# Two trunk layers on one core: six of branch D's eight gate products put between the attention's steps, their logits parked in DRAM, and D's remaining products put together

## The chip, the cores and the metric

One core of one Trainium2 chip runs the whole kernel. The metric is the device time of one execution in microseconds, as the median of the runs shown. TensorE is written PE, VectorE DVE, ScalarE ACT and SyncE SP, as the profile does; GpSimd does nothing here beyond two memsets at the start.

## The reference, cut to what matters

Two layers are applied to 640 tokens (512 latent, 128 context). In each layer one wide projection of the normed input `h` feeds four mixers; each mixer's output is projected to the model's width and weighted by a gate that is computed from the same `h`:

```
z = h @ p['w_in']                       # the last 4 * 1024 columns are merge_logits
y_a, y_c   attention (A: 4 heads of 64; C: differential, 8 score maps of 32)
y_b, y_d   chunkwise linear attention (HGRN2, GLA)
branches = jnp.stack([y_a, y_b, y_c, y_d], axis=2)
proj  = jnp.einsum('btnw,nwd->btnd', branches, p['w_branch'])
gates = jax.nn.sigmoid(merge_logits.reshape(bsz, t, N_BRANCH, D_MODEL))
mixed = jnp.sum(gates * proj, axis=2) @ p['w_out']
x = x + g1 * mixed
x = x + g2 * conv_ffn(...)
```

A gate of one branch for 128 output channels is a product of 1024 x 128 weights with `h` (8 blocks of 128 in depth); the branch's projection for these channels is a product over 256 (2 blocks). `y_d` is the last branch to be ready. The gates of D need only `h`, which is ready before the attention.

## The kernel before

Channels lie on the 128 partitions, the 640 tokens along the free axis. The kernel is written by hand, engine by engine, with semaphores; nothing is scheduled by a compiler, and each engine works through its instructions in the order of the code. For each of two layers: the projections of the mixers (`z`), the attention, then the stage in which B and D are computed while PE fills its waits with the gate and branch products of A, C and B (24 "mix" units, `MERGE`), then D's own gates and branches ("D's stage"), the output projection (`out`), and the ConvFFN (`up`, `down`).

A product is done in split precision: each weight block and each input block is a rounded part ("hi") plus the rest ("lo"), and `block_product` (L571 to L573) issues hi x hi, hi x lo and lo x hi for each of two halves of 320 tokens, six matmuls for a block of depth. So a gate is 48 matmuls of 320 columns, a D branch product 12. For every weight unit ACT makes the hi part (`mix_unit` L1137, `out_unit` L1216) and DVE the lo part (`lo`, L1432) before PE can start on it. Weights come by SP's queue through a ring of four slots (`RING`); SP waits for a free slot before each load, and what stands behind that wait on the queue waits too.

The attention has 30 steps `g` in a layer (five blocks of 128 queries, six steps each: two for A, four for C); the last six have 128 keys only, the others 768. `scores` (L712, L714) writes two score maps into two PSUM pairs and waits until ACT has taken the two maps of the step before. `maxima` (DVE L1511), `exponentials` (ACT L1114), `normalise` (DVE L1518 to L1524), `turn` (PE transposes, L725), `keep_turned` (ACT L1124) and `weigh` (PE, probabilities times values, L739) follow at a distance of up to three steps. In one step PE issues scores(g), turn(g-3, second map), turn(g-2, first map), weigh(g-3); DVE issues maxima(g), then normalise(g-1). `outputs` (L1529) copies the attention's result out of PSUM. `ATT_OUT` takes both banks of the fourth pair.

D's stage before: for each `j` of eight groups of 128 channels PE does the gate and then the branch product; ACT takes the sigmoid from PSUM (L1231); DVE multiplies (`merge`, L1704), adds it to the sum (L1710), ACT rounds that (`round_mixed`, L1235) and DVE makes its rest (`mixed_rest`, L1715). The `out` products read the rounded sum and the rest.

## Time and profile before

| | before |
|---|---|
| median of 3 runs | 2751.46 us (2750.52 to 2757.59) |
| the profiled execution: time, span | 2750.94 us, 2749.2 us |
| mean granted clock of TensorE | 0.956 |
| attention, layer 0: first maxima to last step with 768 keys | 333.61 to 461.33 us |
| D's stage, layer 0 | 788.48 to 858.88 us |
| `out` products, layer 0 | 858.88 to 915.30 us |

Times in the rows are microseconds from the first instruction. In a timeline row stand the start, the duration, the engine and line, what is written and read, how many instructions are merged, and in square brackets how long the engine sat idle before it and what it had waited for. PE's matmuls overlap, so its own pace is read from start to start. A window row gives busy time (and instruction counts) of PE, weight loads, DVE, ACT and POOL, then the granted clock, the DMA share and GB/s.

### The profile page before, as it was taken

What the parts mean: (1) busy time and instruction counts of PE and PEld (TensorE: products, weight loads), DVE (VectorE), ACT (ScalarE), POOL (GpSimd) and SP (SyncE); (2) the same over time, 40 slices, a digit from 0 to 9 for tenths busy, and PEclk for the clock granted to TensorE, in tenths of its full rate; (3) what the DMA queues carried; (4) which work ended last, traced back from release to release, by engine and by line L of the source; (5) the groups of instructions that cost most, each with busy time, mean ns of one, the idle gap of its engine ahead of it and who ended that gap; (6) DMA issues with size and microseconds to landing.
All of it is one profiled execution on the core that took longest, in us unless ns stands there. A gap on an engine that the chain in (4) does not pass through costs nothing.

```text
span 2749.2 us, 43334 instructions
## 1 busy us (share of the span) xinstructions
PE 2541.6 (92%) x18502; PEld 2356.8 (86%) x18502; DVE 1336.9 (49%) x2037; ACT 939.9 (34%) x1306; POOL 2.2 (0%) x6
## 2 busy tenths in 40 slices
PE   4999877999999899998989997879999989999898
PEld 2988655888999899998989884568899989999898
DVE  3123266886644545554231324678775445555521
ACT  4134345222142532333242434542213334233411
POOL 0000000000000000000000000000000000000000
PEclk7999878999999999999999997999999999999999
DMA  8445200221233122222244340011222322222121
GB/s 292 156 143 183 82 1 1 52 54 50 58 99 102 55 70 76 76 62 81 74 146 127 100 144 26 1 29 49 51 63 72 121 62 62 77 76 72 54 74 70
DMA packets 322759, 222.77 MB, mean 81 GB/s; under 512 B 17520, under 2 KB 320688, under 8 KB 321712
## 3 DMA queue, kind: packets, MB, share of 16 engines
q1 hardware_dynamic: 317200, 203.45, 25.4%
q10 hardware_dynamic: 5408, 17.13, 1.7%
q8 instruction: 116, 1.90, 0.3%
q14 instruction: 35, 0.29, 0.0%
HBM read 211.51 MB, written 9.04 MB: 80 GB/s over the span
## 4 chain that ended last, share of the span: by engine, by line
PE 85%; DVE 5%; ACT 5%; issue 2%; DMA 1%; SPq 0%; ACTq 0%; POOLq 0%; DVEq 0%; POOL 0%
PE PS L571 23%; PE PS L573 23%; PE PS L572 23%; PE PS L817 3%; PE PS L739 2%; PE PS L712 2%; PE PS L725 2%; PE PS L595 2%; PE PS L560 1%; DVE RING_split L1432 1%; PE PS L714 1%; ACT HH_split L983 1%; PE PS L853 1%; DVE NMX L1511 1%; ACT WORK L985 1%
## 5 line engine op out<-in xcount | busy, mean ns | idle before, releaser
L571 PE MATMUL PS<-HH_split,WHI_split 128*128 128x320 f32 x3552 | 1119.7, 315 | 44.7 <-DVE HL_split L1418 17.7
L573 PE MATMUL PS<-HH_split,RING_split 128*128 128x320 f32 x3552 | 1103.6, 311 | 0.0
L572 PE MATMUL PS<-HL_split,WHI_split 128*128 128x320 f32 x3296 | 1024.5, 311 | 0.0
L571 PEld LDWEIGHTS PS<-HH_split,WHI_split 128*128 128x128 f32 x3552 | 673.0, 189 | 66.9 <-issue 57.3
L573 PEld LDWEIGHTS PS<-HH_split,RING_split 128*128 128x128 f32 x3552 | 672.6, 189 | 0.0
L572 PEld LDWEIGHTS PS<-HL_split,WHI_split 128*128 128x128 f32 x3296 | 625.1, 190 | 2.4 <-issue 2.4
L1432 DVE TENSOR_TENSOR RING_split<-RING,WHI_split 128x1024 fp32r<-128x1024 f32 (+2 forms) x200 | 274.4, 1373 | 499.7 <-ACT WHI_split L1220 230.6
L572 PE MATMUL PS<-ZT_split,WHI_split 128*128 128x320 f32 x1216 | 378.0, 311 | 0.0
L572 PEld LDWEIGHTS PS<-ZT_split,WHI_split 128*128 128x128 f32 x1216 | 230.6, 190 | 0.0
L1220 ACT ACTIVATE WHI_split<-RING 128x1024 fp32r<-128x1024 f32 x88 | 93.3, 1060 | 290.6 <-PE PS L573 290.6
L571 PE MATMUL PS<-V_split,WHI_split 128*128 128x320 f32 x544 | 172.3, 317 | 19.9 <-DVE ZT_split L1787 15.1
L1439 DVE TENSOR_TENSOR RING_split<-RING,WHI_split 128x1024 fp32r<-128x1024 f32 x54 | 64.2, 1222 | 250.1 <-ACT WHI_split L1001 250.0
L573 PE MATMUL PS<-V_split,RING_split 128*128 128x320 f32 x544 | 170.3, 313 | 0.0
L1511 DVE TENSOR_REDUCE NMX<-PS 128x1 f32<-128x768 f32 (+1 forms) x120 | 93.3, 819 | 102.2 <-PE PS L714 91.7
L1173 ACT ACTIVATE WHI<-PS 128x640 f32<-128x640 f32 x48 | 33.9, 705 | 280.6 <-PE PS L573 280.4
L1114 ACT ACTIVATE BIG<-PS,NMX 128x768 f32<-128x768 f32 (+1 forms) x120 | 94.1, 791 | 88.3 <-DVE NMX L1511 88.3
L571 PEld LDWEIGHTS PS<-V_split,WHI_split 128*128 128x128 f32 x544 | 104.3, 192 | 22.2 <-issue 20.8
L1591 DVE COPY_PREDICATED BIG<-MASK,PS 128x640 f32<-128x640 uint8 x112 | 98.1, 882 | 51.8 <-PE PS L817 51.0
L1224 ACT ACTIVATE WHI_split<-RING 128x1408 fp32r<-128x1408 f32 x32 | 44.2, 1380 | 226.0 <-PE PS L573 226.0
L1137 ACT ACTIVATE WHI_split<-RING 128x1280 fp32r<-128x1280 f32 x64 | 81.5, 1273 | 83.0 <-PE PS L573 83.0
L712 PE MATMUL PS<-ZT 32*128 32x512 f32 (+1 forms) x192 | 65.0, 758 | 45.3 <-ACT BIG L1114 44.0
L573 PEld LDWEIGHTS PS<-V_split,RING_split 128*128 128x128 f32 x544 | 104.3, 192 | 0.0
(181 smaller groups left out, 2781.8 us busy)
## 6 DMA issues: line engine op xcount, KB each, us to landing
RING<-in_w_in SPq DMA_DIRECT2D x112, 512.0 KB, 4.0
RING<-in_w_ada SPq DMA_DIRECT2D x96, 512.0 KB, 6.0
RING<-in_w_up SPq DMA_DIRECT2D x88, 512.0 KB, 5.0
RING<-in_w_down SPq DMA_DIRECT2D x32, 384.0 KB, 3.6
RING<-in_w_down SPq DMA_DIRECT2D x32, 320.0 KB, 4.0
RING<-in_w_branch SPq DMA_DIRECT2D x64, 128.0 KB, 4.1
RING<-in_w_out SPq DMA_DIRECT2D x16, 512.0 KB, 4.1
x_kept<-BIG ACTq DMA_DIRECT2D x2, 2560.0 KB, 9.8
```

The costliest lines, as they stand in the source:

```text
L571: release(pe.matmul(out, w_hi, hi[:, a:b], start=begin, stop=False), fresh and a == 0)
L572: pe.matmul(out, w_hi, lo[:, a:b], start=False, stop=False)
L573: ins = pe.matmul(out, w_lo, hi[:, a:b], start=False, stop=end)
L712: pe.matmul(pair(m)[:, 0:TS], ZT[r[m], q, ti], ZT[r[m], k, 0:TS], start=True, stop=True)
L817: last = pe.matmul(pair(3 - e)[:, ti], KM[p % 2][r, ti], QM[p % 2][r, ti], start=True, stop=True)
L1114: act.activation(PROB[g % 3][m][:, 0:n], pair(m)[:, 0:n], ACT.Exp, bias=NMX[:, g % 3, m:m + 1], accum_out=SUMS[:, g % 3, m:m + 1]).then_in ...
L1137: act.activation(W2[m % 2][:, 0:1280], RING[:, (MIX + m) % N_SLOT, 0:1280], ACT.Copy).then_inc(hi_made, 1)
L1220: act.activation((w or W2[h])[:, 0:1024], RING[:, (UP + j) % N_SLOT, 1024 * h:1024 * h + 1024], ACT.Copy).then_inc(hi_made, 1)
L1432: nv.tensor_tensor(rest, value, as_f32(hi), ALU.subtract).then_inc(lo_made, 1)
L1439: nv.tensor_tensor(z_raw(RING_R, l, c, j), z_raw(RING, l, c, j), as_f32(tiles_of(W4[u % LEAD])), ALU.subtract).then_inc(lo_made, 1)
L1511: nv.tensor_reduce(NMX[:, g % 3, m:m + 1], pair(m)[:, 0:keys(g // NS) * P], AX.X, ALU.max, negate=True).then_inc(nmax_ready, 1)
L1591: ins = nv.copy_predicated(SCORE[:, h], m, ps)
```

## The change

- The gates of D for the first six channel groups (`N_EARLY`) are computed during the attention. `gate_parts` splits each into two halves of 320 tokens, each a chain of 8 units of three matmuls, accumulated in `HALF_GATE`, 320 columns of the second bank of the fourth pair. `GATE_FILL` says how many units PE issues at two places of a step: 2, 6, 2 and 6 units in four steps, 96 units over the 24 steps with 768 keys. ACT copies each half (the logits, no sigmoid yet) to SBUF (`gates_kept`), and PE waits for that copy (`half_kept`) before it begins the next half.
- SP stores each gate's logits to DRAM (`send_gate`), and loads the six back near the end of D's computation.
- The attention's outputs share the first bank of that pair; `weigh` of A waits for `outputs` of the C part before it, and of C for those of A.
- In the attention the transposes run one step earlier: turn(g-2, second), weigh(g-3), turn(g-1, first); DVE does normalise(g-1) before maxima(g). DVE also makes the lo part of a gate's weights (`early_lo`), ACT the hi part (`early_unit`).
- D's stage is ten products: two gates (groups 6 and 7), then eight branch products from two 512-column loads of `w_branch`. The gates that come from DRAM get their sigmoid in SBUF. `merge` no longer has weights to split between its two operations, and SP starts to load `w_out` only when `merge` has used the four gates that lie in the ring (`gate_used`).
- The first two `out` products run together, block by block (`two_products`), and wait for the lo part of the second one's weights. `out` has three hi buffers instead of two.

```diff
+GATE_FILL = ((0, 2), (4, 2), (1, 1), (1, 5))
...
+def halves_before(g):
+    return min(2 * N_EARLY, sum(sum(GATE_FILL[i % 4]) for i in range(g)) // KT)
...
-        ATT_OUT = PS[:, 3, :].rearrange("p (b a t) -> p b a t", b=2, t=P)
+        ATT_OUT = PS[:, 3, 0:512].rearrange("p (b a t) -> p b a t", b=2, t=P)
+        HALF_GATE = PS[:, 3, 512:512 + HALF]
...
+                gate_chunk(LAST, 6)
+                sp.wait_ge(ko_turned, l * 6 + 6)
+                for n in range(N_EARLY):
+                    sp.wait_ge(gate_sent[n], l * 16 + 16)
+                    sp.dma_start(GATE_D[n], LOGITS[:, n, :]).then_inc(gates_in, 16)
+                gate_chunk(LAST + 1, 7)
...
+                sp.wait_ge(gate_used, l * 4 + 4)
                 for c in range(4):
                     slot_free(OUT + c)
                     columns(w_out, (OUT + c) % 4, 256 * c, 256)
...
+                def gate_parts():
+
+                    for n in range(N_EARLY):
+                        w_hi, w_lo = tiles_of(W_EARLY), raw(RING_R, EARLY + n, 0, P, P, KT)
+                        for h, (a, b, _) in enumerate(HALVES):
+                            if h == 0:
+                                lo_ready(U_MIX + n)
+                            if n + h:
+                                pe.wait_ge(half_kept, l * 2 * N_EARLY + 2 * n + h)
+                            for k in range(KT):
+                                release(pe.matmul(HALF_GATE, w_hi[:, k, :], h_hi(k)[:, a:b], start=k == 0, stop=False), h + k == 0)
+                                pe.matmul(HALF_GATE, w_hi[:, k, :], h_lo(k)[:, a:b], start=False, stop=False)
+                                ins = pe.matmul(HALF_GATE, w_lo[:, k, :], h_hi(k)[:, a:b], start=False, stop=k == KT - 1)
...
-                    if g >= 3:
-                        turn(g - 3, 1)
-                    if 0 <= g - 2 < NG:
-                        turn(g - 2, 0)
-                    if g >= 3 and (g - 3) % NS not in (2, 4):
-                        weigh(g - 3)
+                    turn(g - 2, 1)
+                    weigh(g - 3)
+                    gate_fill(g, 0)
+                    turn(g - 1, 0)
+                    gate_fill(g, 1)
...
+                for j in range(KT):
+                    g, at = G_D + 2 + j, j % 4 * P
+                    wait_room(pe, l, g)
+                    if j % 4 == 0:
+                        lo_ready(U_D + 2 + j // 4)
+                    product(use(g)[0], tiles_of(W2[j // 4][:, 0:1024], 512)[:, :, at:at + P], raw(RING_R, LAST + 2 + j // 4, at, P, 512, 2),
...
+                lo_ready(U_OUT + 1)
+                two_products(G_OUT, [out_weights(0), out_weights(1)], m_ready, m_hi, m_lo)
...
+                        if h and n + 1 < N_EARLY:
+                            early_unit(n + 1)
+                        if n == 4 and h == 0:
+                            act.wait_ge(gate_sent[0], l * 16 + 16)
+                        act.activation(LOGIT[n][:, HALVES[h][0]:HALVES[h][1]], HALF_GATE, ACT.Copy).then_inc(half_kept, 1)
...
                 for j in range(KT):
-                    gate(j, 0)
-                    wait_event(act, l, EV_D + 2 * j + 1)
-                    if j < 6:
-                        mix_unit(N_IN + j + 2)
-                    else:
-                        out_unit(j - 6)
+                    if j % 4 == 3:
+                        wait_event(act, l, EV_D + 2 + j)
+                        out_unit(j // 4)
                     round_mixed(j, M_HI[j])
...
                 v.wait_ge(al_ready, l * 2 + 2)
+                early_lo(0)
+                early = 1
                 for g in range(NG + 1):
-                    if g < NG:
-                        maxima(g)
-                    if g >= NS and g % NS == 3:
+                    while early < N_EARLY and 2 * early <= halves_before(g - 1):
+                        early_lo(early)
+                        early += 1
+                    if g % NS == 5:
+                        outputs(g // NS, 0)
+                    if g > NS and g % NS == 3:
                         outputs(g // NS - 1, 1)
                     if g:
                         normalise(g - 1)
-                    if g % NS == 5:
-                        outputs(g // NS, 0)
+                    if g < NG:
+                        maxima(g)
...
+                    step.mark(nv.tensor_tensor(GATED, GATE_D[j], acc(p), ALU.mult))
+                    step.settle(v)
+                    v.sem_inc(gemm_free[p], 1)
+                    if j < 4:
+                        v.sem_inc(gate_used, 1)
                     link(nv.tensor_tensor(dst, dst, GATED, ALU.add))
...
                 for j in range(KT):
                     merge(j)
+                    if j % 4 == 3:
+                        out_lo(j // 4)
                     mixed_rest(j, M_HI[j])
+                out_lo(2)
```

On PE, step g = 4 of the attention before holds the scores, two transposed maps and one product with the values:

```order
L712 MATMUL PS<-ZT 128x512 x2
L714 MATMUL PS<-CACHE,ZT 128x256 x2
L725 MATMUL PS<-CONST,BIG 128x128 x12
L739 MATMUL PS<-WHI,V 64x128 x8
L739 MATMUL PS<-WHI,CACHE 64x128 x4
```

and the same step now:

```order
L762 MATMUL PS<-ZT 128x512 x2
L764 MATMUL PS<-CACHE,ZT 128x256 x2
L793 MATMUL PS<-WHI,V 64x128 x8
L793 MATMUL PS<-WHI,CACHE 64x128 x4
L777 MATMUL PS<-CONST,BIG 128x128 x6
L807 MATMUL PS<-HH_split,WHI_split 128x320
L808 MATMUL PS<-HL_split,WHI_split 128x320
L809 MATMUL PS<-HH_split,RING_split 128x320
L807 MATMUL PS<-HH_split,WHI_split 128x320
L808 MATMUL PS<-HL_split,WHI_split 128x320
L809 MATMUL PS<-HH_split,RING_split 128x320
```

Two units of a gate end the step, and one of the two maps is turned in another step than before. On DVE, the same place before is maxima(4), then normalise(3):

```order
L1511 TENSOR_REDUCE NMX<-PS 128x1 x2
L1518 RECIPROCAL RCP<-SUMS 128x2
L1523 TENSOR_SCALAR BIG<-BIG,RCP,NLAM 128x768
L1524 SCALAR_TENSOR_TENSOR BIG<-BIG,RCP 128x768
```

and now, from maxima(4) to maxima(5):

```order
L1624 TENSOR_REDUCE NMX<-PS 128x1 x2
L1545 TENSOR_TENSOR RING_split<-RING,WHI_split 128x1024
L1645 COPY ZT<-PS 128x2x128
L1634 RECIPROCAL RCP<-SUMS 128x2
L1639 TENSOR_SCALAR BIG<-BIG,RCP,NLAM 128x768
L1640 SCALAR_TENSOR_TENSOR BIG<-BIG,RCP 128x768
L1624 TENSOR_REDUCE NMX<-PS 128x1 x2
```

The lo part of the second gate's weights (L1545) stands behind maxima(4), though PE's step 4 above already reads it; normalise(4) stands ahead of maxima(5). On DVE in D's stage, two groups of channels before:

```order
L1704 TENSOR_TENSOR WORK<-WHI,PS 128x640
L1432 TENSOR_TENSOR RING_split<-RING,WHI_split 128x1280
L1710 TENSOR_TENSOR ZT<-ZT,WORK 128x640
L1715 TENSOR_TENSOR ZT_split<-ZT,V_split 128x640
L1704 TENSOR_TENSOR WORK<-WHI,PS 128x640
L1432 TENSOR_TENSOR RING_split<-RING,WHI_split 128x1280
L1710 TENSOR_TENSOR ZT<-ZT,WORK 128x640
L1715 TENSOR_TENSOR ZT_split<-ZT,V_split 128x640
```

and now groups 2 and 3:

```order
L1831 TENSOR_TENSOR WORK<-RING,PS 128x640
L1836 TENSOR_TENSOR ZT<-ZT,WORK 128x640
L1841 TENSOR_TENSOR ZT_split<-ZT,V_split 128x640
L1831 TENSOR_TENSOR WORK<-RING,PS 128x640
L1836 TENSOR_TENSOR ZT<-ZT,WORK 128x640
L1545 TENSOR_TENSOR RING_split<-RING,WHI_split 128x8x128
L1841 TENSOR_TENSOR ZT_split<-ZT,V_split 128x640
```

The splits between the multiplications and the additions are gone, but that of `w_out` for the first `out` product (L1545 with 128x8x128) stands inside the chain at group 3, ahead of the rest of the sum.

## Rows read from the trace of the kernel before

**Rows 1.** The page: its head and its first part.

```profile
span 2749.2 us, 43334 instructions
...
PE 2541.6 (92%) x18502; PEld 2356.8 (86%) x18502; DVE 1336.9 (49%) x2037; ACT 939.9 (34%) x1306; POOL 2.2 (0%) x6
```

**Rows 2.** Windows of layer 0: attention's first twelve steps, D's stage, `out`.

```profile
330.90:368.74 37.84, 24.77 (x130) 14.68 (x127) 19.50 (x29) 17.25 (x34) 0.00 (x0) 0.67 0.03 11
368.74:399.60 30.86, 24.59 (x192) 16.64 (x193) 21.12 (x33) 16.86 (x33) 0.00 (x0) 0.89 0.00 1
...
788.48:858.88 70.40, 70.40 (x483) 70.40 (x482) 32.45 (x35) 25.58 (x29) 0.00 (x0) 1.00 0.42 132
858.88:915.30 56.42, 56.42 (x386) 56.30 (x384) 22.37 (x30) 14.27 (x16) 0.00 (x0) 1.00 0.26 75
```

**Rows 3.** Timeline of one attention step, all engines.

```profile
404.93 1.13 PE L712 MATMUL PS<-ZT 64*128 64x512 f32 x4
...
406.43 0.87 PE L725 MATMUL PS<-CONST,BIG 128*128 128x128 f32 x6
406.53 1.82 DVE L1511 TENSOR_REDUCE NMX<-PS 128x1 f32<-128x768 f32 x2 [1.00 <-PE PS L714]
...
409.45 1.13 PE L712 MATMUL PS<-ZT 32*128 32x512 f32 x4 [2.15 <-ACT BIG L1114]
```

**Rows 4.** Timeline of a step of C: a turned map, normalise, weigh.

```profile
418.13 0.84 PE L725 MATMUL PS<-CONST,BIG 128*128 128x128 f32 x6 [0.99 <-ACT WHI L1124]
418.43 0.15 DVE L1518 RECIPROCAL RCP<-SUMS 128x2 f32<-128x2 f32 x1
...
418.90 1.09 PE L739 MATMUL PS<-WHI,V 128*64 128x128 f32 x16
419.34 1.02 DVE L1524 SCALAR_TENSOR_TENSOR BIG<-BIG,RCP 128x768 f32<-128x768 f32 x1
...
420.37 1.13 PE L712 MATMUL PS<-ZT 32*128 32x512 f32 x4
```

**Rows 5.** PE's timeline where 320-column matmuls meet others.

```profile
507.28 0.31 PE L573 MATMUL PS<-HH_split,RING_split 128*128 128x320 f32 x1
507.52 1.39 PE L817 MATMUL PS<-RING,BIG 64*128 64x128 f32 x20
508.84 0.42 PE L571 MATMUL PS<-HH_split,WHI_split 128*128 128x320 f32 x1
509.09 0.31 PE L572 MATMUL PS<-HL_split,WHI_split 128*128 128x320 f32 x1
```

**Rows 6.** Timeline at the start of the attention.

```profile
332.11 1.47 ACT L1106 ACTIVATE ZT<-BIG 128x640 f32<-128x640 f32 x2 [0.27 <-DVE BIG L1506]
333.61 1.82 DVE L1511 TENSOR_REDUCE NMX<-PS 128x1 f32<-128x768 f32 x2 [0.80 <-ACT ZT L1106]
```

**Rows 7.** Timeline of PE after its long wait behind `out`.

```profile
927.33 0.60 PE L571 MATMUL PS<-HH_split,WHI_split 128*128 128x320 f32 x1 [5.78 <-DVE HL_split L1418]
...
932.97 0.30 PE L571 MATMUL PS<-HH_split,WHI_split 128*128 128x320 f32 x1
```

**Rows 8.** Timeline of DVE and ACT in D's stage.

```profile
797.63 0.82 DVE L1704 TENSOR_TENSOR WORK<-WHI,PS 128x640 f32<-128x640 f32 x1 [2.32 <-PE PS L573]
...
800.27 0.82 DVE L1710 TENSOR_TENSOR ZT<-ZT,WORK 128x640 f32<-128x640 f32 x1
801.95 0.83 DVE L1715 TENSOR_TENSOR ZT_split<-ZT,V_split 128x640 fp32r<-128x640 f32 x1 [0.86 <-ACT V_split L1235]
...
859.16 1.06 ACT L1216 ACTIVATE WHI_split<-RING 128x1024 fp32r<-128x1024 f32 x1 [1.05 <-PE PS L573]
...
860.25 1.23 DVE L1432 TENSOR_TENSOR RING_split<-RING,WHI_split 128x1024 fp32r<-128x1024 f32 x1 [0.20 <-ACT WHI_split L1216]
```

**Rows 9.** The page: a copy out of PSUM, and loads by SP.

```profile
L1173 ACT ACTIVATE WHI<-PS 128x640 f32<-128x640 f32 x48 | 33.9, 705 | 280.6 <-PE PS L573 280.4
...
RING<-in_w_out SPq DMA_DIRECT2D x16, 512.0 KB, 4.1
```

More of the change, by code:

```diff
@@ L741, in weigh, with gate_fill @@
                     last.then_inc(pv_done, 1)
+                def gate_parts():
+                    for n in range(N_EARLY):
+                        w_hi, w_lo = tiles_of(W_EARLY), raw(RING_R, EARLY + n, 0, P, P, KT)
[8 more added lines that the diff above has]
+                                ins = pe.matmul(HALF_GATE, w_lo[:, k, :], h_hi(k)[:, a:b], start=False, stop=k == KT - 1)
+                                if k == KT - 1:
+                                    ins.then_inc(half_gate, 1)
+                                yield
+                gates = gate_parts()
+                def gate_fill(g, n):
+                    for _ in range(GATE_FILL[g % 4][n]):
+                        next(gates, None)
                 for g in range(NG + 3):
@@ L890, in _, with m_hi, m_lo @@
+                def m_hi(k):
+                    return M_HI[k]
+                def m_lo(k):
+                    return ZT_R[:, MIXT + k, :]
+                lo_ready(U_OUT + 1)
+                two_products(G_OUT, [out_weights(0), out_weights(1)], m_ready, m_hi, m_lo)
+                for t in range(2, 8):
+                    wait_room(pe, l, G_OUT + t)
+                    lo_ready(U_OUT + t)
+                    product(use(G_OUT + t)[0], *out_weights(t), m_hi, m_lo, KT, t % 2 == 0)
                 mean_square(1)
```

200 lines of the change are left out of this document (123 added, 77 removed).

## The prediction

> **What bounds the kernel now.** I read the page first: PE is busy for 92% of the span, DVE for half of it [rows 1]. Then the windows by stage. In D's stage and in `out` PE is busy without a gap at the full clock; in the attention the granted clock is 0.67 in the first six steps and 0.89 in each later six [rows 2]. So what D's stage loses in PE work it can lose in time, as long as nothing else becomes late there, and the attention is the place with slack. How much, the step's timeline tells: scores start at 404.93, the next at 409.45, and PE had sat idle for 2.15 us, waiting for ACT's second map [rows 3]. These 4.5 us are a loop of latencies: scores 1.6, two maxima 1.82 with ACT half a map behind, ACT's two maps.
>
> **PE's work in six steps, at full clock.** Scores take 1.5 us (404.93 to 406.43) [rows 3]. A turned map is 0.77 (418.13 to 418.90), a `weigh` 1.47 (418.90 to 420.37) [rows 4]. Six steps hold 6 scores, 8 maps and 4 `weigh`: 9.0 + 6.2 + 5.9 = 21.1 us, in a stretch of 30.86 [rows 2]. Slack 9.8.
>
> **What the fill costs.** D's stage is 480 matmuls of 320 columns in 70.40 us [rows 2], so 0.147 each; a unit of three is 0.44, and six steps get 24 units, 10.6 us. Each group of units put between other matmuls also pays for the meeting: L573 to L817 is 0.24 and L571 to L572 behind it 0.25, against 0.147, so 0.2 for both ends [rows 5]. There are 7 groups in four steps, 10.5 in six: 2.1 us. Together 21.1 + 10.6 + 2.1 = 33.8, above 30.86: **PE becomes the bound of the attention**, and six steps last 2.9 us longer. Below stands 31.7 (+0.8), if the fp32 matmuls of the attention meet the units without a price. The loop that ruled before does not rule any more: from ACT's last map normalise of C takes 1.93 (418.43 to 420.36) [rows 4], then maxima(g) and ACT's maps 2.9, so 4.9 a step at most, against PE's mean of 5.6. A half copy of 320 columns is less than the 0.70 of 640 [rows 9], and ACT does it while PE does the next scores (1.5 us), before the next unit needs the bank; if that cover were gone it would be up to 0.7 for each of 12.
>
> Two smaller terms. (a) DVE makes a gate's lo weights behind maxima(g) of the step whose end PE wants to fill: maxima end 1.6 + 1.8 = 3.4 after the scores began, lo is 1.23 [rows 8], ready at 4.7, while PE is there at 1.5 + 1.47 + 0.77 = 3.7, or at 4.5 where a second map is turned. Of the five places three cost 1.0 and two 0.25: 3.5. (b) At the start `early_unit` (1.06) and `early_lo` (1.23) [rows 8] stand between the last ACT operation of the decays and the first maxima, at 333.61 with no other wait [rows 6]: +2.5, so scores(1) at 339.1. Step 1 holds scores, one map and six units with two meetings: 1.5 + 0.8 + 2.6 + 0.4 = 5.3. Step 2 has two units only, so the loop rules: 4.9. Step 3 has both maps, a `weigh` and six units: 7.6. Step 4 has a map, a `weigh`, two units and 1.0 of (a): 5.8. Step 5 is as step 1: 5.3. Together 28.9, and the clock is low at first. After PE's wait behind `out` it stays at half for 5.64 us of work (927.33 to 932.97, 0.267 a matmul) [rows 7], a loss of at most 2.8; I take 2.2. Then step 6 begins at 370.2, against 368.74: +1.5, with the gain from a clock that was 0.67 in it. The later three stretches: 3 x 2.9 = 8.7, and the other 2.5 of (a). The last, short steps have no units: 0. **Attention: +12.7 us a layer** (between 0, where the clock's gain covers the units, and +16).
>
> **D's stage.** Six gates of 48 matmuls leave it: 288 x 0.147 = 42.2 us of PE. What is late next is DVE. PE's two gates run from 788.48 to 802.6. Then ACT's hi of the second branch chunk (1.06) and DVE's lo (1.23) [rows 8] stand ahead of all merges in DVE's order: first merge at 805.1. A group costs DVE: multiply 0.82, 0.06 to settle, 1.68 from the addition's start to that of the rest (800.27 to 801.95, ACT's rounding in it), 0.75 of the rest: 3.3 us [rows 8]. PE needs 12 x 0.147 = 1.8. Before, a gate's 7 us hid this chain; now it is bare. At group 3 comes a wait: SP loads `w_out` only after merge(3) has multiplied (815.0 + 0.9), each load lands after 4.1 [rows 9] and the second is issued 0.4 later, so 820.5; then ACT's hi to 821.6, DVE's lo to 822.9, the rest to 823.7. Group 4 starts at 823.6 in place of 818.3. ACT and DVE stand in order behind that load, so nothing goes round it. Groups 5, 6 and 7 start at 826.9, 830.2 and 833.5; the addition of 7 ends at 835.2, and then DVE makes the lo part that PE waits for ahead of the first two `out` products: 836.4. PE was last needed at 818, when group 3's multiplication had freed the PSUM pair of group 7. It restarts at 836.5 instead of 858.88: 22.4 us earlier, with 18 us of idleness behind it, so again 2.2 for the clock. Both products then run as before, the remaining six too. **D's stage: -20.2 us a layer.** Bounds: -25.5, if the load were hidden; -17, if the load lands 3 us later.
>
> The Trainium skill (TensorE: Matmul & The Clock Gate, Why this matters for your kernels) says to leave no long idle gaps between bursts, since PE then falls back to the low clock. That speaks against this change, which makes one such gap in D's stage and fills many in the attention; the rows agree (0.89 in the attention, the half-speed start above). By the rule alone the first products of `out` would be slow, which the sum has.
>
> The stores and loads of the logits (six of 320 KB each way) cost nothing: SP has them in stages where DMA share is 0 to 0.4 [rows 2], and the loads are issued when the last group's `KO` is turned, some 30 us ahead of their sigmoid. If they were late, ACT would be, and merge(0) behind it. The sigmoids themselves (0.7 each) end at about 806, as the first merge does. Outputs in one bank add waits of `weigh` for a copy of 0.4 us that DVE has made one step before: 0.
>
> **Sum.** A layer: +12.7 - 20.2 = -7.5; two layers -15.0. The profiled execution took 2750.94 (span 2749.2 [rows 1]), 0.5 below the median. 2750.9 - 15.0 = 2735.9, forecast **2736 us**.
>
> **Rivals.**
> 1. The units go in nearly free: no price for meetings, the higher clock pays the start; +3 a layer in place of +12.7. For it: the clock of 0.67 and 0.89, which leaves 4 to 8 us a layer to win. Against: PE's sum is above the stretch even at full clock. 2750.9 - 2 x 17.2 = 2716.5.
> 2. D's stage stays bound by PE (DVE's chain hidden, `w_out` in time): -42.2 there and +12.7: 2 x -29.5, so 2692. Against: 3.3 us a group in order on DVE against 1.8 on PE. It would need rounding and rest to overlap with the next group's multiplication, which the code's order forbids.
> 3. Slower, by one mechanism: the single bank of the halves. If ACT's copy waits behind its two maps (2 x 0.9 and two read-outs of 0.2) and PE for it, each of 12 boundaries costs 2.2 + 0.5. It decides from 7.5/12 = 0.6 us a boundary on. At 2.0 each: 24 a layer, 2750.9 + 2 x (24 - 7.5) = 2784. Against: in ACT's order the copy stands ahead of the step's maps, and a half ends with a step, so the scores cover it. The Trainium skill (Perfetto Trace Analysis, Matmuls) would expect this cost: "Independent matmul groups should rotate through different PSUM banks", so that the copy of one overlaps the next group's matmuls. No row here shows such a wait.
> 4. No difference: the attention becomes 18 to 22 us longer a layer, because 2, 6, 2, 6 units meet the steps with maps and `weigh` unevenly, so that latencies rule the short steps and PE the long ones (7.6 beside 4.9): 2746 to 2754. If the clock stays at 0.9 as well, 33.8 becomes 37.6 in each of four stretches, 15 a layer: 2766.
>
> **How the numbers follow.** The first sum with its own bounds (attention +9 to +15, D's stage -17 to -22): 0.57, from 2725 to 2746. Rival 1: 0.20. Rival 2: 0.04. Rival 3: 0.05. Rival 4: 0.14. The range of 8 in 10 goes from rival 1's time to just short of rival 4's middle: 2714 to 2750. A difference under 0.3% (8 us) is about what cannot be told from none; the first case reaches a little into it (from 2743 on). Rival 4 gives most of the chance of no difference and 0.03 of slower. Faster 0.78, same 0.14, slower 0.08.
>
> **What would show it.** Right: in the attention a granted clock near 1 and six steps in about 33.8 us, long steps every second, PE's waits small and for DVE's lo weights; in D's stage DVE at 3.3 us a group with one wait of about 5 us for `w_out` at group 3, PE idle for some 18 us ahead of the first `out` product, which starts 48 us after the start of D's stage instead of 70. Wrong: PE idle in the attention for ACT's half copies (rival 3), six steps still in 31 us (rival 1), steps longer than PE's own sum (rival 4), or PE busy through D's stage (rival 2).

## The result, and the profile after

The changed kernel takes 2723.8 us (median of four runs, 2722.7 to 2725.4) against 2751.3 before: a ratio of 0.9895, 95% interval 0.9883 to 0.9907. Forecast were 2736 us and a range of 2714 to 2750. The direction and the range held; the middle was 12 us too high. The kernel before was measured again beside each group of experiments (2753.6 to 2754.9 us), so where two versions differ by a few us their ratios to it say more than their times; one of the four executions of experiment 2, at 5359 us, is twice as long as the other three and is left out of its ratio.

The page of the changed kernel, head and first part, which answer to [rows 1]:

```profile
span 2723.6 us, 43386 instructions
...
PE 2523.2 (93%) x18502; PEld 2344.4 (86%) x18502; DVE 1339.8 (49%) x2041; ACT 948.4 (35%) x1334; POOL 2.2 (0%) x6
```

PE's matmuls are the same 18502 instructions, in 25.6 us less. Windows of layer 0, which answer to [rows 2]: the attention in four stretches of six steps, D's stage up to the first `out` product, and from there to PE's first product behind `out` (3.7 us of it a wait; measured to the same place, 919.12, the kernel before took 60.2 us where [rows 2] has 56.42). Columns: stretch, its length, busy time and number of instructions of PE, weight loads, DVE, ACT and POOL, granted clock, DMA share, GB/s.

```profile
329.72:369.11 39.39, 32.91 (x210) 23.87 (x210) 23.58 (x34) 23.21 (x41) 0.00 (x0) 0.87 0.16 46
369.11:401.38 32.27, 32.27 (x265) 25.02 (x264) 22.68 (x34) 19.05 (x37) 0.00 (x0) 1.00 0.09 28
401.38:435.43 34.05, 32.51 (x265) 24.99 (x264) 23.93 (x35) 20.15 (x38) 0.00 (x0) 1.00 0.21 59
435.43:467.70 32.27, 32.27 (x266) 25.01 (x265) 22.67 (x34) 19.05 (x37) 0.00 (x0) 1.00 0.11 32
796.86:846.28 49.42, 28.67 (x195) 28.14 (x193) 28.42 (x35) 21.28 (x28) 0.00 (x0) 0.85 0.38 132
846.28:909.04 62.76, 59.08 (x385) 58.84 (x385) 22.07 (x32) 15.27 (x18) 0.00 (x0) 0.96 0.24 68
```

In two of the three later stretches of the attention PE is now busy from end to end, at a granted clock of 1.00, where it was 0.89 in [rows 2]. A stretch grew from 30.9 us to 32.3 (34.1 in the third, which has two waits for weights). D's stage gives its time back: 49.4 us to the first `out` product in place of 70.4. Of these, PE works 28.7. PE's waits in the attention, in the changed kernel (who waited for whom, us in total, times, the longest):

```profile
PE PS L807 <- DVE RING_split L1545: 6.3, 4, 4.0
PE PS L759 <- ACT BIG L1220: 1.4, 3, 0.7
PE PS L762 <- ACT BIG L1220: 1.2, 2, 0.8
```

L807 is the first matmul of a unit, RING_split the lo part of its weights. It waits for DVE's lo weights and never for ACT's copy of a finished half. The 4.0 us are the first gate's, at the start; the three others are 0.8 each. Two smaller waits of PE (for a kept map and for the decays) are not shown.

DVE's, ACT's and SP's timeline in D's stage of the changed kernel, at group 3, with the restart of PE:

```profile
823.91 0.81 DVE L1831 TENSOR_TENSOR WORK<-RING,PS 128x640 f32<-128x640 f32 x1
824.90 3.56 SPq L486 DMA_DIRECT2D RING<-in_w_out  x6
824.96 0.83 DVE L1836 TENSOR_TENSOR ZT<-ZT,WORK 128x640 f32<-128x640 f32 x1 [0.24 <-DVE WORK L1831]
829.99 1.06 ACT L1329 ACTIVATE WHI_split<-RING 128x1024 fp32r<-128x1024 f32 x1 [6.85 <-DMA RING<-in_w_out]
831.15 1.23 DVE L1545 TENSOR_TENSOR RING_split<-RING,WHI_split 128x1024 fp32r<-128x1024 f32 x1 [5.36 <-ACT WHI_split L1329]
...
833.03 0.81 DVE L1831 TENSOR_TENSOR WORK<-WORK,PS 128x640 f32<-128x640 f32 x1
...
845.01 1.22 DVE L1545 TENSOR_TENSOR RING_split<-RING,WHI_split 128x1024 fp32r<-128x1024 f32 x1
...
846.28 0.64 PE L621 MATMUL PS<-V_split,WHI_split 128*128 128x320 f32 x1 [19.43 <-DVE RING_split L1545]
```

It reads from the top: group 3 has multiplied, SP may load `w_out` (824.90), it lands 5.1 us later, ACT makes hi, DVE has stood for 5.36 us and makes lo, and group 4 starts at 833.03. PE has stood for 19.43 us when the second unit's lo is there.

**Where the 25.6 us of span came from**, by the places where PE starts a stage in both traces (`ffn` is PE's first block product behind `out`):

| stretch | layer 0: before, after | layer 1: before, after |
| --- | --- | --- |
| decays' product to first mix product (attention) | 157.26, 162.73: +5.5 | 158.00, 162.43: +4.4 |
| first mix product to the second pause of the mix stage | 157.21, 159.37: +2.2 | 157.32, 157.25: -0.1 |
| from there through D's stage and `out` to `ffn` | 287.73, 268.53: -19.2 | 287.60, 268.57: -19.0 |

These sum to -26.2, and the rest of the span adds 0.6. Of the gain in the last row 18.5 and 18.1 us lie in D's stage and `out`, the rest behind them. The two layers do not divide the attention's growth alike: in layer 0 the part up to the seventh scores is 0.4 us shorter and the three later stretches are 6.0 longer; in layer 1 they are 2.2 and 3.8 longer (one of the stretches before lasted 33.0 there, at a clock of 0.84), and what follows them is 1.5 shorter.

### The profile page after: what moved, and what is told of

Same layout as the page of the kernel before. It is cut to its first block, busy times and chain, and to the rows that moved or that the text cites. A ratio compares the mean times of both kernels' runs of the same rounds, so it can differ in the third digit from the quotient of the medians.

```text
span 2723.6 us, 43386 instructions
## 1 busy us (share of the span) xinstructions
PE 2523.2 (93%) x18502; PEld 2344.4 (86%) x18502; DVE 1339.8 (49%) x2041; ACT 948.4 (35%) x1334; POOL 2.2 (0%) x6
## 4 chain that ended last, share of the span: by engine, by line
PE 83%; DVE 7%; ACT 6%; issue 2%; DMA 1%; SPq 0%; ACTq 0%; POOLq 0%; DVEq 0%; POOL 0%
PE PS L621 22%; PE PS L622 21%; PE PS L623 21%; PE PS L896 2%; PE PS L762 2%; DVE RING_split L1545 2%; PE PS L645 2%; PE PS L777 2%; PE PS L793 2%; PE PS L807 1%; PE PS L610 1%; ACT HH_split L1070 1%; ACT WORK L1072 1%; PE PS L809 1%; PE PS L808 1%
## 5 line engine op out<-in xcount | busy, mean ns | idle before, releaser
L621 PE MATMUL PS<-HH_split,WHI_split 128*128 128x320 f32 x3360 | 1061.2, 316 | 45.1 <-DVE HL_split L1531 18.3
L623 PE MATMUL PS<-HH_split,RING_split 128*128 128x320 f32 x3360 | 1044.4, 311 | 0.0
L622 PE MATMUL PS<-HL_split,WHI_split 128*128 128x320 f32 x3104 | 965.6, 311 | 0.0
L621 PEld LDWEIGHTS PS<-HH_split,WHI_split 128*128 128x128 f32 x3360 | 637.0, 190 | 68.4 <-issue 57.2
L623 PEld LDWEIGHTS PS<-HH_split,RING_split 128*128 128x128 f32 x3360 | 636.8, 190 | 0.0
L622 PEld LDWEIGHTS PS<-HL_split,WHI_split 128*128 128x128 f32 x3104 | 589.2, 190 | 2.4 <-issue 2.4
L1545 DVE TENSOR_TENSOR RING_split<-RING,WHI_split 128x1024 fp32r<-128x1024 f32 (+2 forms) x204 | 274.9, 1349 | 535.6 <-ACT WHI_split L1333 240.8
L1248 ACT ACTIVATE WHI_split<-RING 128x1280 fp32r<-128x1280 f32 (+1 forms) x56 | 69.5, 1241 | 78.1 <-PE PS L623 78.1
L1898 DVE SCALAR_TENSOR_TENSOR WORK<-PS,COLS,WORK 128x511 f32<-128x511 f32 (+1 forms) x176 | 88.6, 545 | 10.8 <-DVE WORK L1894 2.1
```

The costliest lines, as they stand in the source:

```text
L621: release(pe.matmul(out, w_hi, hi[:, a:b], start=begin, stop=False), fresh and a == 0)
L622: pe.matmul(out, w_hi, lo[:, a:b], start=False, stop=False)
L623: ins = pe.matmul(out, w_lo, hi[:, a:b], start=False, stop=end)
L1248: act.activation(W2[m % 2][:, 0:width], RING[:, (MIX + m) % N_SLOT, 0:width], ACT.Copy).then_inc(hi_made, 1)
L1545: nv.tensor_tensor(rest, value, as_f32(hi), ALU.subtract).then_inc(lo_made, 1)
L1898: ins = nv.scalar_tensor_tensor(out=c[:, a:b - 1], in0=u[:, a + 1:b], scalar=COLS[:, bass.ds(col + C_W2, 1)], in1=c[:, a:b - 1], op0=ALU.m ...
```

## The experiments

**1. Loads by slot.** Each chunk of `w_out` waits only for the gate that lies in its own slot; the four gates that come back into the ring are put in the slots in which `w_out` will arrive in order.

```
-        GATE_D = [RING[:, b, 1280:1280 + T] for b in range(4)] + ...
+        GATES_D = [[RING[:, (CHUNK0[l] + C_OUT + b) % N_SLOT, 1280:1280 + T] for b in range(4)] + ...
...
-                sp.wait_ge(gate_used, l * 4 + 4)
                 for c in range(4):
+                    sp.wait_ge(gate_used, l * 4 + c + 1)
```

> Edit: the four gates that lie in the ring are put where the four w_out chunks will go, in the order in which they are used, and each w_out load waits for its own slot's gate alone (chunk c for merge(c)), not for all four. Theory (the chain on DVE rules D's stage, with one wait of about 5.6 us for w_out at group 3): the first load starts behind merge(0) instead of merge(3), is there long before group 3, group 4 starts some 5.3 us earlier and so do the out products: out starts about 44 us after the start of D's stage in place of 49.4, 2 x 5.3 = 10.6 us in all, 2713. Rival (out's start is set by something else, ACT's hi parts or the PSUM pairs): out starts at 49 us again, 2724.

Measured: 2713.0 us, ratio 0.985 (0.9834 to 0.9867). D's stage up to the first `out` product, by windows, 5.3 us shorter:

```profile
795.43:839.53 44.10, 28.67 (x195) 28.14 (x194) 28.43 (x35) 21.16 (x28) 0.00 (x0) 0.90 0.43 148
```

So the wait for `w_out` at group 3 stood on the path with its whole length, 10.6 us in two layers, and it is avoidable.

**2. The second unit of `w_out` two groups earlier,** at group 5, on top of 1 ("version 2" below; the others are numbered alike).

```
-                    if j % 4 == 3:
-                        wait_event(act, l, EV_D + 2 + j)
+                    if j in (3, 5):
+                        wait_event(act, l, EV_D + (5 if j == 3 else 9))
                         out_unit(j // 4)
```

> Edit: on top of the loads by slot, the hi and lo parts of the second out product's weights are made at group 5 of D's stage instead of group 7. Theory: PE waits for that lo part alone, then takes six blocks of the two products whose sums are ready, and the last two are ready by the time it comes to them: out starts two groups earlier (6.8 us), the end of the two products moves as much, 2 x 6.7 = 13 us below the run with the loads by slot, about 2700. Rival (the rounded sums of groups 6 and 7 come too late, so PE only waits inside the products): the end of the two products moves by less than 3 us a layer, 2707 to 2713.

Measured: 2694.9 us, ratio 0.9783 (0.9763 to 0.9802). The same window, and PE's row behind it:

```profile
792.17:829.49 37.32, 28.66 (x195) 28.14 (x193) 23.65 (x29) 19.22 (x25) 0.00 (x0) 0.97 0.49 174
```

```profile
829.49 0.64 PE L622 MATMUL PS<-V_split,WHI_split 128*128 128x320 f32 x1 [7.33 <-DVE RING_split L1546]
```

Another 6.8 us a layer, two groups of DVE at 3.4, so 13.6 in all. The time fell by 18: in the two profiled executions, 16.9 us apart, the rest lies in stretches that the edit doesn't touch and that differ by 0.9 to 1.5 us each, most of them in favour of this version (the stretch from the last pause of the mix stage to D's stage: 150.42 us in version 1, 148.90 here). The restart hung on the place of one lo unit in DVE's order, and not on the mixed tiles: PE takes these one by one.

**3. No fill.** The 96 units run in a row behind the attention.

```
-GATE_FILL = ((0, 2), (4, 2), (1, 1), (1, 5))
+GATE_FILL = ((0, 0),) * 4
```

> Edit: no unit of a gate stands between the attention's steps, all 96 run behind the last step. Theory (with units PE's own sum rules the steps, without them the loop of latencies does, 4.5 us where the step before is A's and 4.9 where it is C's): six steps last 28.5 us in place of 32.9 with the units and 30.9 before the change. The 96 units take 42 us plus a bare copy of a half (0.7) at 12 places and bare hi and lo parts (2.4) at 5: 63. So +45 a layer, about 2815. Rival (the new order of transposes and normalise gives nothing): six steps take 31 us as before the change, about 2835.

Measured: 2850.8 us (two runs), ratio 1.0351 (1.0327 to 1.0375), 36 us more than expected. Windows of the later three stretches:

```profile
367.74:400.35 32.61, 26.39 (x193) 17.21 (x193) 21.50 (x33) 16.96 (x33) 0.00 (x0) 0.84 0.00 1
400.35:429.14 28.79, 21.71 (x192) 14.36 (x192) 21.41 (x33) 16.84 (x33) 0.00 (x0) 1.00 0.01 1
429.14:461.77 32.63, 26.42 (x193) 17.24 (x193) 21.50 (x33) 16.97 (x33) 0.00 (x0) 0.84 0.01 1
```

The 28.5 us that I expected of six empty steps are there once (28.8), at the full clock; in the two others the clock was 0.84 and they take 32.6, as long as six steps filled with 24 units (32.3). From the first scores to the twenty-fifth, the layer is 131.96 us without units and 137.98 with them: 42 us of PE's work are done for 6. The kernel before took 132.18, so the new order in the steps by itself shortened nothing. The rest of the miss is the row of units: 461.77 to the first mix product at 552.74 is 90.97 us, against 20.90 in the changed kernel, so 70 for the units, with 2.4 us for the lo weights of each gate but the first and half clock behind four of these five pauses:

```profile
514.95 0.64 PE L807 MATMUL PS<-HH_split,WHI_split 128*128 128x320 f32 x1 [2.40 <-DVE RING_split L1545]
```

**4. One place a step.** The same units, 4.5 meetings fewer in six steps.

```
-GATE_FILL = ((0, 2), (4, 2), (1, 1), (1, 5))
+GATE_FILL = ((0, 2), (0, 6), (0, 2), (0, 6))
```

> The changed kernel with the numbers of units per place at 0,2 | 0,6 | 0,2 | 0,6 in place of 0,2 | 4,2 | 1,1 | 1,5: the same 24 units in six steps, but one group of units a step instead of up to two, so 4.5 meetings fewer in six steps. Theory (a meeting of units with the attention's matmuls costs PE about 0.04 us): between -2 and +2 us over the whole kernel, 2724. Rival (0.2 us each, as predicted): 4.5 x 0.2 = 0.9 us less in each of the stretches, 3.6 a layer, so 7 us faster, 2717. A small loss would come from steps in which PE has nothing to put before the second turned map and waits for it.

Measured: 2723.4 us, ratio 0.9892 (0.9876 to 0.9909): no difference from the changed kernel. Windows of the three later stretches:

```profile
368.94:401.31 32.37, 32.09 (x265) 24.81 (x265) 22.97 (x34) 19.13 (x37) 0.00 (x0) 1.00 0.11 28
401.31:435.15 33.84, 32.29 (x265) 24.81 (x264) 23.64 (x35) 19.73 (x37) 0.00 (x0) 1.00 0.21 59
435.15:467.51 32.36, 32.07 (x265) 24.79 (x265) 22.97 (x34) 19.14 (x37) 0.00 (x0) 1.00 0.11 32
```

They sum to 98.6 us, as in the changed kernel. PE's busy time in the three fell from 97.05 to 96.45, 0.60 for 13.5 meetings: 0.04 each. (A meeting is one group of units between other matmuls.) Even that is not saved, since PE now stands as long elsewhere, twice for a normalised map (0.3 each):

```profile
PE PS L777 <- DVE BIG L1640: 0.6, 2, 0.3
```

As a net price of a meeting the rival's 0.2 is out; what the 0.04 is made of stands in the section on the prediction.

**5. Four units in every step.**

```
-GATE_FILL = ((0, 2), (4, 2), (1, 1), (1, 5))
+GATE_FILL = ((0, 4), (2, 2), (1, 3), (1, 3))
```

> Edit: the 96 units are spread evenly, four in each step, instead of 2, 6, 2, 6. Theory (a step lasts as long as the longer of PE's work and the loop of 4.5 to 4.9 us): the light steps (one map, no weigh) have 4.1 us of PE work and fall under the loop, the heavy ones get longer, six steps 33.3 in place of 32.1 (without the waits for lo weights): +4.7 a layer, about 2733. Rival (the unevenness of the steps, 4.7 beside 7.3, is what costs time against PE's sum): six steps get shorter, down to 31.7, about 2718.

Measured: 2727.8 us (two runs), ratio 0.9904 (0.9884 to 0.9924), between the two expectations. It is 4 us above the changed kernel, but the intervals of the two ratios overlap, so only the windows can tell them apart. The first of its later stretches, and PE's waits in the three of them:

```profile
365.82:398.89 33.07, 32.38 (x264) 24.99 (x264) 22.72 (x34) 19.03 (x37) 0.00 (x0) 1.00 0.09 27
```

```profile
PE PS L762 <- ACT BIG L1220: 2.0, 6, 0.3
PE PS L807 <- DVE RING_split L1545: 1.8, 2, 1.0
```

Six times PE waits 0.3 us for ACT's exponentials in a step of 4.51 us, the shortest there is: steps with one map and no `weigh` have too little work with four units. The changed kernel has six there and no such wait in these stretches. They sum to 101.2 us in place of 98.6; the first stretch is 1.6 shorter. The uneven 2, 6, 2, 6 of my rival 4 is thus the better spread in the later stretches; over the whole kernel the runs do not show it.

**6. The copy behind the exponentials,** which is rival 3's mechanism.

```
-                    gates_kept(halves_before(g))
                     keep_turned(g - 2, 1)
                     if g < NG:
                         exponentials(g)
+                    gates_kept(halves_before(g))
```

> The changed kernel with ACT's copy of the finished half of logits behind the step's two exponentials instead of ahead of them. This makes the third rival of the prediction true on purpose. Theory (the single bank of halves costs nothing only because ACT copies while PE does the scores): the copy is made about 2.2 us later, so PE, which wants the bank at once behind the scores and the turned map, waits about 1.8 to 2.0 us at each of 12 half boundaries: about 42 us in two layers, 2766. Rival (the place of the copy doesn't matter, since units have other slack): 2724.

Measured: 2811.7 us (two runs), ratio 1.0211 (1.0191 to 1.0232), 88 us slower than the changed kernel. PE's waits over the stretch that was shown above for the changed kernel:

```profile
PE PS L807 <- DVE RING_split L1545: 15.2, 5, 4.0
PE PS L807 <- ACT WORK L1211: 10.0, 5, 3.0
```

PE waits 2.0 us for a copy on average, as expected, at five places. What I had left out: the call that I moved also makes the next gate's hi weights, so at the four other places DVE's lo comes late (2.8 us on average); and the granted clock over 329 to 380 us is 0.71 where the changed kernel has 0.87 over its first six steps. So the experiment moves two things, and its 88 us are not the price of the copy alone. The place of this call decides between 28 us gained and 58 lost.

**7. Maxima first,** DVE's order of before.

```
+                    if g < NG:
+                        maxima(g)
                     if g % NS == 5:
                         outputs(g // NS, 0)
...
                     if g:
                         normalise(g - 1)
-                    if g < NG:
-                        maxima(g)
```

> The changed kernel with DVE's order in a step of the attention as it was before the change: maxima of this step ahead of the normalising of the step before. Theory (with units between, PE no longer waits for the exponentials but for the normalised map, which it turns in the same step; with the maxima ahead it comes 1.8 us later, and the PE's mean step of 5.4 us has no room for that): about 9 us more in each six steps, 72 in two layers, 2796. Rival (the order is free, since PE has units to do while DVE works): under 10 us more, 2724 to 2734.

Measured: 2833.3 us (two runs), ratio 1.029 (1.0269 to 1.031): 110 us slower than the changed kernel, where 72 were expected. PE's waits from 330 to 480 us:

```profile
PE PS L777 <- DVE BIG L1640: 18.9, 10, 3.4
PE PS L777 <- DVE BIG L1637: 6.4, 5, 2.0
```

L777 turns a map, L1637 and L1640 normalise it. The fifteen waits are 1.7 us each on average, as the theory said (1.8); the first to the twenty-fifth scores (328.5 to 514.6 us) take 186.1 us in place of 138.0. Over all of it the waits for a map sum to 30.8 us, those of `weigh` for DVE's `outputs`, which now stand behind the maxima, to 4.6, and the clock is 0.78, 0.89, 0.96 and 0.96 in the four stretches; the expectation had counted the first of these alone. With units in the steps, DVE's new order is a condition of the gain.

**8. The second unit at group 4,** on top of 2.

```
-                    if j in (3, 5):
-                        wait_event(act, l, EV_D + (5 if j == 3 else 9))
+                    if j in (3, 4):
+                        wait_event(act, l, EV_D + (5 if j == 3 else 9))
```

> On top of the version with w_out loaded slot by slot and the second unit of w_out at group 5: now that unit's hi on ACT and its lo on DVE stand at group 4. Theory (PE's restart in D's stage is set by where DVE makes the second unit's lo weights, and DVE's order of groups at 3.4 us each does the rest): out starts 3.4 us earlier a layer (its pause of 7.3 us becomes 3.9), and each k step of the first two products still finds its mixed tile ready, since they take 1.8 us each (3.5 while PE is at half clock) and the last rest comes at 837: 2 x 3.4 = 6.8 us faster than the version before it, about 2688 us. Rival (the tiles of groups 5 to 7 come too late for a PE that starts earlier, so the pause is only moved between the k steps): no gain, 2695.

Measured: 2695.2 us, ratio 0.9789 (0.9772 to 0.9805): no gain over 2. The window and PE's row:

```profile
792.92:828.59 35.67, 28.67 (x195) 28.17 (x194) 22.86 (x28) 18.63 (x24) 0.00 (x0) 0.99 0.52 182
```

```profile
828.59 0.61 PE L622 MATMUL PS<-V_split,WHI_split 128*128 128x320 f32 x1 [5.67 <-DVEq L1834]
```

Neither theory. The lo was ready, but PE then waited for something else (DVEq L1834, the settling behind a group's multiplication): the second `out` product needs the PSUM pair that group 5 frees. That gave 1.65 us in place of 3.4, and 0.7 more behind it, a layer. In the profiled execution these 4.7 us were lost again in stretches that the edit doesn't touch; the longest loss is behind a short pause, at half clock here and not in version 2 (1480.57 to 1518.01, 37.44 us, in version 2; 1478.77 to 1517.76, 38.99, here). Why they fall in one version and not in the other is not shown: the four executions of this version lie within 1.1 us of each other and the three of version 2 within 1.4, so it is not chance from one execution to the next. The intervals of the two ratios are wide enough to hold a gain of 4.7.

**9. One gate back in D's stage,** behind the first four branch products, on top of 8; the 80 units that are left are spread over twelve steps.

```
-N_IN, N_EARLY = 24, 6
+N_IN, N_EARLY = 24, 5
...
-GATE_FILL = ((0, 2), (4, 2), (1, 1), (1, 5))
+GATE_FILL = ((0, 2), (4, 2), (1, 1), (1, 1), (2, 2), (0, 6), (0, 2), (4, 2), (1, 1), (0, 0), (0, 2), (4, 2))
...
                 for j in range(KT):
+                    if j == 4:
+                        wait_room(pe, l, G_D + 6)
+                        lo_ready(U_D + 3)
+                        product(use(G_D + 6)[0], tiles_of(W2[1][:, 0:1024]), raw(RING_R, LAST + 3, 0, P, P, KT), h_hi, h_lo, KT, True)
```

> On top of the version with the second unit of w_out at group 4: five gates of branch D in the attention in place of six, the sixth again in D's stage, but behind the first four branch products, where PE waits for DVE's groups anyway. The attention's 80 units are spread over twelve steps so that no step with two turned maps or a weigh has more than four, and every half still ends with a step. Theory (the attention is bound by PE, so a unit that leaves it gives back its full 0.44 us, and D's stage has PE idle for about 7 us, so the gate's 7.04 us of matmuls fit there at little cost): attention -7.0 us a layer; in D's stage DVE makes one more lo unit in its chain (+1.2) and ACT one more hi, the out product starts at about 37 to 38 us after the stage's start as before, the pause of 5.7 us is nearly gone and with it up to 2.5 us of half clock. Together -7 to -8 a layer, 2 x -7.5 = -15: 2680 us. Rival (the latencies of the attention's steps rule as soon as they hold fewer units, as in the version without any fill, whose six steps were no shorter than those of the changed kernel): attention -1 to -2 a layer and D's stage +1: 2695.

Measured: 2698.0 us, ratio 0.9796 (0.978 to 0.9813). D's stage holds a whole gate more and lasts 2.25 us longer than in version 8, as expected:

```profile
793.93:831.85 37.92, 35.44 (x243) 35.18 (x241) 24.79 (x30) 20.26 (x26) 0.00 (x0) 1.00 0.54 185
```

But a pause is left at the restart, and PE's pace is halved for 3.4 us soon behind it, no less than in version 8 (2.4 to 2.6), so the half clock that I wanted to save is still there:

```profile
831.85 0.41 PE L626 MATMUL PS<-V_split,WHI_split 128*128 128x320 f32 x1 [2.48 <-DVE RING_split L1561]
...
832.86 0.47 PE L628 MATMUL PS<-V_split,RING_split 128*128 128x320 f32 x1
```

The attention gave nothing: decays' product to first mix product is 161.49 us, against 161.50 in version 8. PE's waits there, and one of them with the matmuls behind it:

```profile
PE PS L812 <- DVE RING_split L1561: 10.0, 4, 4.0
```

```profile
442.63 0.42 PE L812 MATMUL PS<-HH_split,WHI_split 128*128 128x320 f32 x1 [3.04 <-DVE RING_split L1561]
...
443.56 0.47 PE L814 MATMUL PS<-HH_split,RING_split 128*128 128x320 f32 x1
```

A matmul record of a unit is 0.31 us long at full clock and 0.47 at half. The pause of 3 us is followed by half clock, and that step takes 9.67 us where its like take 5.0.

**10. Other places for the gates' starts,** on top of 9: every gate begins behind maps and `weigh`; the last four steps are empty.

```
+GATE_FILL = ((0, 2), (4, 2), (1, 3), (1, 3), (0, 2), (4, 2), (1, 1), (1, 5), (0, 4), (1, 3), (1, 1), (1, 5),
+             (0, 2), (4, 2), (1, 3), (1, 3), (0, 2), (4, 2), (1, 1), (1, 5), (0, 0), (0, 0), (0, 0), (0, 0))
```

> On top of the version with the sixth gate back in D's stage: the same 80 units, but at other places. In that version three gates began in steps where PE has little else to do (2.3 us of scores and one turned map, or units ahead of the turned map), and PE waited 2.24, 0.77 and 3.04 us for DVE's lo weights, each followed by half clock (steps of 8.9, 6.3 and 9.7 us where 5.0 would do). Here every gate begins in a step whose scores, maps and weigh take 3.8 us and behind them, as in the changed kernel (a wait of 1.0 at most), and the last four steps are empty. Theory (where a gate begins is what took the gain of the fewer units): scores to first mix product about 4 us a layer shorter than before this edit, since 7.0 us of units are gone and about 3 us are lost again to the latencies of the two empty light steps: 2 x -4 = -8, 2690 us. Rival (fewer units buy nothing, because the loop of latencies takes over step by step): the same time as the version before it, 2697.

Measured: 2701.6 us, ratio 0.9809 (0.9793 to 0.9826). Windows: the last steps with scores of full width, and from there to the first mix product.

```profile
428.69:462.88 34.19, 30.17 (x249) 21.90 (x248) 24.37 (x36) 19.52 (x39) 0.00 (x0) 1.00 0.13 40
462.88:485.77 22.89, 16.29 (x102) 10.45 (x103) 11.99 (x38) 9.88 (x36) 0.00 (x0) 0.53 0.01 1
```

The theory holds as far as it went: the first to the twenty-fifth scores take 134.1 us, 4.3 less than in version 9. But behind the empty steps the clock is 0.53, and the next stretch takes 22.89 us where version 9 has 19.86 at 0.74; the first mix products take 16.05 us, against 14.85. What the lighter attention gave, the clock took.

## Why the prediction was right, and where its size was off

**What bounds, and D's stage.** Right in nearly every step. First merge 16.6 us after the stage's start, as predicted. A group takes DVE 3.48 us in place of 3.3 (the settling is 0.24, I had 0.06), and 3.38 from group 4 on. The wait for `w_out` came at group 3 and is 5.4 us (5.3 predicted). PE restarts 49.4 us after the stage's start, predicted 48.0, with 19.4 us of idleness behind it (18), and is at half clock for 5.5 us. From D's stage to `ffn` the gain is 19.2 and 19.0 us, predicted 20.2; 18.5 and 18.1 of it lie where I had put all of it. Rival 2, a stage bound by PE, is out: PE works 28.7 of the 49.4 us. Experiments 1 and 2 show that the two causes of its pause, the late load and the place of a lo unit, were worth 10.6 and 13.6 us by the windows (the times moved by 11 and 18). What running the first two `out` products together is worth by itself, no run shows.

**The attention.** The mechanism was right: PE is its bound, and its granted clock is full from the second stretch on. The size was not. Predicted +12.7 us a layer, measured +5.5 and +4.4. The step of the prediction that failed is this one: "L573 to L817 is 0.24 and L571 to L572 behind it 0.25, against 0.147, so 0.2 for both ends", added to "A turned map is 0.77". The term was laid on each of 10.5 groups of units, on top of pieces whose lengths I had read beside other neighbours. Six steps filled without a wait take 32.27 us; my sum of PE's work without meetings was 31.7, so a meeting adds 0.05 us net, and experiment 4 gives 0.04. PE's timeline of the changed kernel shows why it is so little:

```profile
394.66 0.41 PE L807 MATMUL PS<-HH_split,WHI_split 128*128 128x320 f32 x1
394.91 0.31 PE L808 MATMUL PS<-HL_split,WHI_split 128*128 128x320 f32 x1
395.06 0.31 PE L809 MATMUL PS<-HH_split,RING_split 128*128 128x320 f32 x1
395.20 0.82 PE L777 MATMUL PS<-CONST,BIG 128*128 128x128 f32 x6
395.78 0.39 PE L807 MATMUL PS<-HH_split,WHI_split 128*128 128x320 f32 x1
396.00 0.31 PE L808 MATMUL PS<-HL_split,WHI_split 128*128 128x320 f32 x1
396.15 0.31 PE L809 MATMUL PS<-HH_split,RING_split 128*128 128x320 f32 x1
396.39 1.13 PE L762 MATMUL PS<-ZT 32*128 32x512 f32 x4
```

The first two starts of a unit are 0.25 and 0.22 us apart and the scores start 0.24 behind the last one, as in [rows 5]; only the exit to a map is free (395.06 to 395.20). A group so costs 0.10 to 0.17 more than its units, not 0.05. But the map between two groups takes 0.58 (395.20 to 395.78), where I had read 0.77 in front of a `weigh` [rows 4]. In the stretch from 369.11 to 401.38 the 24 units with their 11 groups take 12.2 us (12.7 by my terms), the eight maps 5.3 (6.2), scores and `weigh` 14.8 (14.9). So the maps, counted too long, are the larger part of the miss of 1.5 a stretch and the price of a meeting the smaller.

Of the miss in layer 0 the three later stretches hold 5.2 us (6.0 measured, 11.2 predicted), 4.6 of it this (3 x 1.5) and the rest DVE's lo weights, 0.8 at two places in place of 1.0 and nothing at two where I had 0.25. The start holds 1.9 (-0.4 from the decays' product to the seventh scores, 43.61 us before and 43.24 after, where +1.5 was predicted); 1.4 of these lie in steps one to five, 31.1 us predicted and 29.7 measured; how they divide between maps, meetings and the clock stays open. In layer 1 the start was not too high (+2.2 measured), the later stretches grew by 3.8, and what follows them, put at 0, gave back 1.5 us.

**How near the forecast came.** For the span I had -15.0 and it is -25.6. I had the cost of the attention 15.5 us too high in both layers, the gain of D's stage and what follows 2.2 too large, and 2.7 of loss in no term. The last two worked against the first and brought the forecast nearer, which is luck.

**Costed at nothing.** Rightly so: logits out and back (no row waits for them), outputs in one bank. The half copies cost nothing because of their place; rival 3's condition was right. Experiment 6 has 3.3 us a boundary (first to twenty-fifth scores 178.2 us in place of 138.0, 12 boundaries) where rival 3 had 2.7, but that holds the late hi weights and the lower clock too; the wait for the copy alone was 2.0. The Trainium skill (Perfetto Trace Analysis, Matmuls) wants independent groups in different banks. Experiment 6 agrees with its reason; the changed kernel shows that the scores between two groups can give the same cover (no wait for a copy).

**Rivals.** Rival 1 (units nearly free, +3 a layer) was closer in its time than the forecast (2716.5 and 2736, measured 2723.8), and it had named both reasons: no price for meetings, and a clock that rises as the units go in. Experiment 3 shows the second: without units, two of three stretches fall to 0.84. The other rule that the prediction weighed, of the Trainium skill (TensorE: Matmul & The Clock Gate, Why this matters for your kernels), against long idle gaps, agrees with the rows on both sides: half clock for 5.5 us behind the gap made in D's stage, and full clock where gaps were filled. Pauses of 1.70 us, below, are short and yet some are followed by half clock. The PE sum that I set against rival 1 held (31.7, and no filled stretch is shorter than 32.3), but it stands only 0.8 above the old stretch. Rival 4 fell with the windows: PE is busy through 32.27 of 32.27 us, short steps (4.7 and 5.0 us) and long ones alike, where it had latencies rule the short ones.

**Not in the sum.** 2.2 us in layer 0's mix stage, against us, and -0.1 in layer 1's. PE's row there, of the changed kernel and then of the one before:

```profile
572.07 2.50 PE L894 MATMUL PS<-ZT,WORK 64*128 64x128 f32 x20 [1.70 <-issue]
```

```profile
565.19 1.39 PE L815 MATMUL PS<-ZT,WORK 64*128 64x128 f32 x20 [1.70 <-issue]
```

The same twenty matmuls behind the same pause of 1.70 us take 2.50 in one and 1.39 in the other, and the stage is 1.5 us longer from there to the next pause (75.90 against 74.41). In layer 1, and in versions 2 and 8, that stretch takes 74.4; in experiment 5 it takes 75.9 in layer 0 too. What decides whether the clock falls behind a pause of this length stays open; PE's instructions there are the same in both kernels.

## What to carry to other kernels

Work moved into a stage where the engine waits costs less than its own length, since it fills the waits and here also raised the granted clock (0.89 to 1.00): 42 us of matmuls for about 6. Work taken out again gave nothing back here, in experiment 9 because gates then began where their weights were not ready, in 10 because the clock was low behind the empty steps. After such a move look first at the chain that it laid bare, here the position of one load's condition and of one lo unit in DVE's order, which were worth nearly as much again as the change: 24 us by the windows, 29 by the times (version 2: 2695).

## What the runs showed of the hardware

- A group of the 320-column matmuls between fp32 ones costs PE 0.10 us more than its units where a map follows and 0.17 where scores follow, but the map between two groups is 0.57 us long in place of the 0.80 that one takes in front of a `weigh` (380.28 to 381.08 in the changed kernel). Net this is 0.04 to 0.05 a group. A length that was read beside one neighbour does not hold beside another.
- The granted clock fell behind pauses of 2.2, 2.5, 3.0 and 19.4 us, and behind one of 1.70 us in layer 0 of the changed kernel but not in its layer 1. That last fall costs 1.5 us, and profiles of two versions differ by as much at places that the edit doesn't touch (experiments 2 and 8).
- `w_out` landed 4.4 us after its issue (median) with its loads let go one by one, 6.5 where three of the four chunks of a layer were let go together (4.1 before, [rows 9]).
